# Three edits in a one-core transformer kernel: the last expert's scatter, the squares of an attention, the gate rows of a scan

## The reference, cut to what matters

```python
# first block: for each head and direction, chunk by chunk (here 128 tokens)
logw = where(tril, cum[..., :, None] - cum[..., None, :] + ic[..., None, :], -inf)
m = maximum(inter, logw.max(-1))
s = einsum('bhjd,bhsd->bhjs', qc, kc) * exp(logw - m[..., None])
...
# experts: 16 experts, each takes its 128 best tokens
y = einsum('becf,efd->becd', hid, w_down) * vals[..., None]
return zeros_like(h).at[bidx, idx].add(y)
...
# first attention ("A"): 4 heads, two softmaxes each, then a norm over the 128 values of a head
w = p[:, :, 0] - lam * p[:, :, 1]
o = rms_norm(einsum("bhqk,bkhe->bqhe", w, v), subln_g) * (1.0 - lam_init)
```

## Time and profile before

| | us |
|---|---|
| median of 3 runs | 3016.61 (3014.56 to 3016.85) |
| the profiled execution, its time | 3016.07 |
| its span in the trace | 3014.2 |
| PE busy in it | 2781.5 |
| DVE busy | 1690.4 |
| ACT busy | 1408.7 |

### The profile page before, as it was taken

How to read it: one execution, slowest core, us unless ns; L and a number is a source line. 1 busy time by engine, 2 the same in 40 slices (tenths; PEclk the granted TensorE clock), 3 DMA queues, 4 the chain that set the end, 5 groups by cost and what they waited for, 6 DMA issues and landing times.

```text
span 3014.2 us, 38322 instructions
## 1 busy us (share of the span) xinstructions
PE 2781.5 (92%) x13952; PEld 2070.1 (69%) x13966; DVE 1690.4 (56%) x3155; ACT 1408.7 (47%) x2556; POOL 211.7 (7%) x250
## 2 busy tenths in 40 slices
PE   7999999999993899999978988999999989989998
PEld 3567794788772677777747755675677775866676
DVE  2368363334467788888846468544533556536533
ACT  2343362223242666666636356634632548437421
POOL 0000000000010000000015000000020000000500
PEclk9999999999996999999989999999999999999999
DMA  9510200322434899999965000301041201000321
GB/s 374 190 56 29 102 11 1 135 89 84 156 143 166 306 378 378 377 377 378 377 181 161 17 22 8 85 1 43 23 133 68 86 15 58 29 18 19 113 84 56
DMA packets 178537, 401.33 MB, mean 133 GB/s; under 512 B 7964, under 2 KB 9020, under 8 KB 177872
## 3 DMA queue, kind: packets, MB, share of 16 engines
q1 hardware_dynamic: 158224, 329.27, 30.8%
q0 software_dynamic: 20016, 70.00, 7.2%
q10 hardware_dynamic: 144, 0.01, 0.0%
HBM read 363.44 MB, written 35.81 MB: 132 GB/s over the span
## 4 chain that ended last, share of the span: by engine, by line
PE 80%; DVE 8%; ACT 5%; issue 4%; DMA 3%; POOL 0%; DVEq 0%; POOLq 0%; SPq 0%; ACTq 0%
PE psum L787 7%; PE psum L302 7%; PE psum L789 7%; PE psum L788 7%; PE psum L1490 4%; PE psum L1492 4%; PE psum L1491 4%; PE psum L1625 4%; PE psum L1435 3%; PE psum L1434 3%; PE psum L1433 3%; PE psum L1667 3%; PE psum L1643 3%; PE psum L1728 2%; PE psum L1730 2%
## 5 line engine op out<-in xcount | busy, mean ns | idle before, releaser
L788 PE MATMUL psum<-ring_r,kctx_r 128*128 128x512 f32 (+1 forms) x544 | 214.0, 393 | 0.0
L788 PE MATMUL psum<-ring_r,cols_r 128*128 128x512 f32 (+1 forms) x544 | 213.6, 393 | 0.0
L2136 ACT ACTIVATE ring<-ring,att 128x256 f32<-128x256 f32 (+7 forms) x256 | 173.3, 677 | 72.8 <-DVE att L2774 72.8
L2628 DVE TENSOR_TENSOR ring_r<-ring,pair_r 128x1024 fp32r<-128x1024 f32 x128 | 148.0, 1219 | 51.4 <-ACT pair_r L2014 51.4
L1625 PE MATMUL psum<-wide 64*128 64x512 f32 (+2 forms) x704 | 152.8, 515 | 18.5 <-DVE att L2774 15.5
L1491 PE MATMUL psum<-ring_r,wide_r 128*128 128x512 f32 x384 | 151.3, 394 | 0.0
L626 DVE TENSOR_TENSOR ring_r<-ring,ring_r 128x1024 fp32r<-128x1024 f32 x48 | 58.7, 1225 | 129.7 <-ACT ring_r L623 129.3
L1433 PE MATMUL psum<-small_r,ring_r 128*128 128x512 f32 x320 | 125.8, 393 | 0.8 <-DVE pair L2498 0.8
L1435 PE MATMUL psum<-small_r,ring_r 128*128 128x512 f32 x320 | 126.3, 395 | 0.0
L2014 ACT ACTIVATE pair_r<-ring 128x1024 fp32r<-128x1024 f32 x128 | 124.6, 1049 | 0.0
L788 PEld LDWEIGHTS psum<-ring_r,kctx_r 128*128 128x128 f32 x544 | 104.9, 193 | 22.5
(11 more groups left out here) (557 smaller groups left out, 7185.0 us busy)
## 6 DMA issues: line engine op xcount, KB each, us to landing
ring<-in_w_gate SPq DMA_DIRECT2D x64, 1024.0 KB, 9.5
ring<-in_w_up SPq DMA_DIRECT2D x32, 1024.0 KB, 9.7
hidden<-in_w_up SPq DMA_DIRECT2D x32, 1024.0 KB, 9.6
hidden<-in_w_down SPq DMA_DIRECT2D x32, 1024.0 KB, 8.8
pair<-in_w_down SPq DMA_DIRECT2D x32, 1024.0 KB, 9.0
ring<-in_w_ada SPq DMA_DIRECT2D x24, 1024.0 KB, 14.4
ring<-in_w_in SPq DMA_DIRECT2D x24, 1024.0 KB, 7.3
ring<-in_even_w_in SPq DMA_DIRECT2D x16, 1024.0 KB, 13.6
```

What stands on the lines that cost most here:

```text
L788: self.eng.matmul(outp, XHIGH[b][:, k, :], low[:, k, 0:wd], start=False, stop=False)
```

## The change

It has three parts. (1) The last expert's result goes out in one transfer of full rows, with the same code as the other experts (`one(NEXP, False)`). (2) In attention A ACT squares one block in each step, right after the exponentials (`square(g)`), instead of eight at the end of a head; the square root stays behind the eighth. The sums lie in two halves of `qst`, for even and odd heads. (3) The gate rows are split into a float32r part `r_high` (rows 0 to 35 of `extra`) and the rest `r_low` (rows 64 to 99), and one float32r product with the doubled selector (100 x 128) takes the place of the float32 product with 36 rows. For it the constant `sel` becomes 100 rows high, ACT copies it once to float32r, DVE clears `extra` ahead of the wait for `gates`, and DVE makes `r_low`.

```diff
--- before.py
+++ after.py
@@ -173,14 +173,16 @@
                    ("wide", 9256),
                    ("small", 6500),
                    ("kctx", NH * CTX), ("cols", NCH * 4 * NG),
-                   ("sel_wT", 8 * P), ("lam_f", 448), ("dftc", 2 * P + 1))
+                   ("sel_wT", 8 * P), ("lam_f", 448), ("dftc", 2 * P + 1), ("extra", SEQ))
         with ExitStack() as views:
             split = {n: views.enter_context(nc.sbuf_tensor(n + "_r", [P, c], F32R)) for n, c in REGIONS}
-        ring, hidden, ctx_hidden, pair, wide, small, kctx, cols, sel_wT, lam_f, dftc = (sb(n, c) for n, c in REGIONS)
+        ring, hidden, ctx_hidden, pair, wide, small, kctx, cols, sel_wT, lam_f, dftc, extra = (sb(n, c) for n, c in REGIONS)
         ident = sb("ident", P)
         identb = sb("identb", P, BF16)
         maskb = sb("maskb", 2 * NH * P, BF16)
-        sel = sel_wT[0:NG, :]
+        NB = 64 + NG
+        sel_both = split["sel_wT"][0:NB, :]
+        sel = split["sel_wT"][0:NG, :].bitcast(F32)
         cT = sb("cT", KT * 2)
         adaT = sb("adaT", 2 * 48)
         badaT = sb("badaT", 48)
...
@@ -446,7 +447,7 @@
         se = small[:, 3336:3336 + 1024].rearrange("p (b h n) -> p b h n", b=2, h=NH)
         ee = small[:, 4360:4360 + 1024].rearrange("p (b h n) -> p b h n", b=2, h=NH)
         obs = [small[:, o:o + NH * VW].rearrange("p (h n) -> p h n", h=NH) for o in (5384, 5984)]
-        rRs = extra[0:NG, :]
+        r_high, r_low, r_both = (split["extra"][q, :] for q in (slice(0, NG), slice(64, NB), slice(0, NB)))
         dnb = lam_f[:, 256:256 + 8 * NCH].rearrange("p (c n) -> p c n", c=8)
         rec = small[:, 5980:5984]
         oT = pair[:, 0:4 * D].rearrange("p (h n) -> p h n", h=NH)
...
@@ -935,7 +936,7 @@
         @block.gpsimd
         def _(pool):
             for o, i in ((badaT[:], a["b_adaT"]), (gT[:], a["gT"]), (ident[:], a["ident"]),
-                         (mask_in, a["masks"]), (sel, a["sel"]),
+                         (mask_in, a["masks"]), (sel_wT[0:NB, :], a["sel"]),
                          (dftc[:], a["dftc"]), (wconv[:], a["w_convT"]), (wgate, a["w_mgate"]),
                          (bgate[0:NG, :], a["b_gate"]), (wrt[:], a["w_routerT"])):
                 pool.dma_start(o, i).then_inc(S("const"), 16)
...
@@ -1005,14 +1006,7 @@
             with pool.Fori(1, NEXP - 1) as e:
                 one(e, True)
             one(NEXP - 1, False)
-            for m in range(2):
-                ms = slice(m * HALF, (m + 1) * HALF)
-                pool.wait_ge(S("moe_y"), 2 * NEXP - 1 + m)
-                pool.tensor_scalar(idx1[:, 2 + m:3 + m], idxc[:, NEXP - 1:NEXP], 2, m, ALU.mult, ALU.add)
-                pool.drain()
-                pool.indirect_dma_start(scratch["acc"].rearrange("t (m n) -> (t m) n", m=2), bass.IndirectOffsetOnAxis(idx1[:, 2 + m:3 + m].bitcast(U32), 0), yb[:, ms], None,
-                                        compute_op=ALU.add).then_inc(S("moe_sct"), 16)
-            pool.wait_ge(S("moe_sct"), 16 * NEXP + 16)
+            one(NEXP, False)
             pool.wait_ge(S("gf"), 16)
             for t in range(TT + 1):
                 if t < TT:
...
@@ -1349,6 +1344,7 @@
             pe.wait_ge(S("v_ev"), NCH)
             pe.wait_ge(S("qk_silu"), 2 * NH)
             pe.wait_ge(S("c_zero"), 2)
+            pe.wait_ge(S("r_low"), 1)
 
             def scan_first(i):
 
...
@@ -1365,7 +1361,7 @@
                     pe.wait_ge(S("scan_e"), 4 * no)
                 pe.matmul(bank(1), identb[:], maskb[:, d * NH * P:(d + 1) * NH * P], start=True, stop=False, skip_group_check=True)
                 for h in range(NH):
-                    mm = pe.matmul(bank(1)[:, span(h)], sel[:, (4 * d + h) * P:(4 * d + h + 1) * P], rRs[:, span(c - CT)],
+                    mm = pe.matmul(bank(1)[:, span(h)], sel_both[:, (4 * d + h) * P:(4 * d + h + 1) * P], r_both[:, span(c - CT)],
                                    start=False, stop=(h == NH - 1), skip_group_check=True)
                 mm.then_inc(S("scan_r"), 1)
                 if no >= 1:
...
@@ -1799,6 +1795,7 @@
                     u_act(i - 2)
                 if i % 2 == 0:
                     ada_act(i + 2)
+            act.activation(sel_both, sel_wT[0:NB, :], ACT.Copy).then_inc(S("sel_mm"), 1)
             NC.squares(act, 0)
             NC.squares(act, 1)
             NC.evac_act(act, 0)
...
@@ -1836,7 +1833,7 @@
                     act.wait_ge(S("fu_ev"), 2 * (c - 1))
                 act.activation(sinp[c % 2], bank(2 * (c % 2) + 1), ACT.Copy).then_inc(S("sinp"), 1)
             act.wait_ge(S("gate_rows"), 1)
-            act.activation(rRs, rR[:, CTX:TTOT], ACT.Copy)
+            act.activation(r_high, rR[:, CTX:TTOT], ACT.Copy).then_inc(S("r_high"), 1)
             for c in range(NCH):
                 act.activation(rF[:, span(c)], rI[:, span(c)], ACT.Exp, bias=stat[0:NG, 20 + c:21 + c])
                 act.activation(rC[:, span(c)], rR[:, span(c)], ACT.Exp, bias=stat[0:NG, 40 + c:41 + c])
...
@@ -2148,15 +2145,19 @@
                     act.activation(wT[wT_of(at, t, h)][:, 0:n, :], turned(i)[:, 0:n * P].rearrange("p (k n) -> p k n", k=n),
                                    ACT.Copy).then_inc(S(name + "_wevA"), 1)
 
-                def squares(c):
-                    act.wait_ge(S("A_o"), before("A_o") + at.last[c] + 1)
-                    for b in range(TT):
-                        if c or b:
-                            act.wait_ge(S("A_osq"), TT * c + b)
-                        act.activation(xsq, obuf[c % 2][:, b, :], ACT.Square,
-                                       accum_out=qst[:, b:b + 1]).then_inc(S("A_osq"), 1)
-                    act.wait_ge(S("A_osq"), TT * (c + 1))
-                    act.activation(qst[:, 8:16], qst[:, 0:8], ACT.Sqrt, bias=epsc[:, 0:1], scale=1.0 / (2 * HD)).then_inc(S("A_ort"), 1)
+                def square(g):
+                    c, b = at.pairs[g][0:2]
+                    q = 24 * (c % 2) + b
+                    act.wait_ge(S("A_o"), before("A_o") + g + 1)
+                    if g:
+                        act.wait_ge(S("A_osq"), g)
+                    if c >= 2:
+                        act.wait_ge(S("A_on"), before("A_on") + c - 1)
+                    act.activation(xsq, obuf[c % 2][:, b, :], ACT.Square, accum_out=qst[:, q:q + 1]).then_inc(S("A_osq"), 1)
+                    if g == at.last[c]:
+                        q = 24 * (c % 2)
+                        act.wait_ge(S("A_osq"), TT * (c + 1))
+                        act.activation(qst[:, q + 8:q + 16], qst[:, q:q + 8], ACT.Sqrt, bias=epsc[:, 0:1], scale=1.0 / (2 * HD)).then_inc(S("A_ort"), 1)
 
                 def mix(c):
                     i = at.turns["fin", c]
...
@@ -2173,8 +2174,8 @@
                         exponentials(e, (1,))
                     if t is not None and at.heads == 2:
                         empty(t, 1)
-                    if name == "A" and at.ended(i, 0) is not None:
-                        squares(at.ended(i, 0))
+                    if name == "A" and u is not None:
+                        square(u)
                     for c in fins:
                         mix(c)
                 act.wait_ge(S(name + "_trD"), before(name + "_trD") + at.wide0[-1])
...
@@ -2355,6 +2356,7 @@
             for t in range(TT):
                 ss.tokens(t)
             link(dve.memset(ones_row, 1.0))
+            link(dve.memset(split["extra"][:].bitcast(F32), 0.0))
             dve.wait_ge(S("gates"), 1)
             link(dve.tensor_scalar(rM, rM, 0.0, None, ALU.min))
             link(dve.tensor_tensor(rF, rM, rC, ALU.subtract))
...
@@ -2405,6 +2407,8 @@
                 dve.tensor_tensor(fuT[:, c, HALF + 1:D][:, ::-1], cosp[:, 1:HALF], half[:, 1:HALF], ALU.subtract).then_inc(S("fu_ev"), 1)
             dve.wait_ge(S("fu_mm"), 5)
             dve.tensor_copy(fuT[:, :, HALF], bank(7)[:, 0:4]).then_inc(S("fu_ev"), 1)
+            dve.wait_ge(S("r_high"), 1)
+            dve.tensor_tensor(r_low, rR[:, CTX:TTOT], r_high.bitcast(F32), ALU.subtract).then_inc(S("r_low"), 1)
             cols_dve(range(NCH))
             dve.wait_ge(S("dn_mm"), before("dn_mm") + 1)
             dve.tensor_copy(dnb, bank(6)[:, 0:8 * NCH].rearrange("p (c n) -> p c n", c=8)).then_inc(S("dn"), 1)
...
@@ -2824,10 +2828,12 @@
 
                 def complete(c):
 
+                    q = 24 * (c % 2)
+                    r = qst[:, q + 16:q + 24]
                     dve.wait_ge(S("A_ort"), c + 1)
-                    link(dve.reciprocal(qst[:, 16:24], qst[:, 8:16]))
+                    link(dve.reciprocal(r, qst[:, q + 8:q + 16]))
                     for b in range(TT):
-                        ins = dve.tensor_scalar(obuf[c % 2][:, b, :], obuf[c % 2][:, b, :], qst[:, 16 + b:17 + b], None, ALU.mult)
+                        ins = dve.tensor_scalar(obuf[c % 2][:, b, :], obuf[c % 2][:, b, :], r[:, b:b + 1], None, ALU.mult)
                     ins.then_inc(S("A_on"), 1)
 
                 def mix(c):
...
@@ -2997,6 +3003,7 @@
```

(23 more changed lines are left out.)

## The result

| | before | after |
|---|---|---|
| median | 3015.59 us (4 runs, 3013.44 to 3016.85) | 2994.18 us (4 runs, 2993.02 to 2996.55) |
| span of the profiled execution | 3014.2 us | 2993.2 us |

The ratio is 0.9927, interval 0.9912 to 0.9942: 22.0 us less by the ratio, between 17.5 and 26.5 (the two medians are 21.4 apart). Forecast were 16.5 less and a time from 2996 to 3012. The kernel is faster, as forecast, and faster than the range allowed.

The account below looks back on a forecast made before the run. PE was taken to bound the scan, with DVE's gate chain on the path ahead of it. Terms -10.3 - 5.0 - 2.5 + 0.6 + 0.7 = -16.5 against 3016.07 made 2999.6, say 3000 us; range 2996 to 3012.

Parts of the forecast that it names:

- the rivals: Short float32r product no faster, 3010.4 (0.33); only the scan gives, 3007.6 (0.10); squares hold up wide steps, 3023 (0.05).
- A: Scan: a short float32r product is no faster than a float32 one, the scan gives 0, 3010.4; chance 0.33.
- Squares, -5.0: Attention A, heads' ends: seven of eight squares go earlier, 1.7 us at each of three ends; bounds 3.2 and 8.2.
- Gate rows on PE, -10.3: Scan: four products per output step fall from 1.08 to 0.44 us, 0.64 saved in each of 16 steps.
- That the saving passes on: Scan: L2460 ends 1.6 us ahead, ACT idles 1.73 a step, so PE stays the bound, period 4.87.
- Its cost ahead, +1.3: Setup ahead of the scan: 0.6 us for DVE's clear and up to 0.7 for the larger selector transfer.
- The clear's 0.6: DVE's clear of `extra` before the wait for `gates` makes PE's wait at L1291 0.6 us longer; bounds 0 and 1.2.
- The selector's 0.7: At the start: the selector's transfer grows from 36 to 100 rows, 262 KB more at 394 GB/s, up to 0.7 us.
- The moved squares cost nothing, narrowly: Attention A, steps with 1024 keys: slack 1.6 us before L2797, use 1.4, 0.2 left; no added table loads.
- Scatter, -2.5: Last expert: one full transfer issued at 1564.9 instead of a second half at 1569.89, 2.5 us gained; bounds 0.4 and 5.0.
- The range: Whole kernel: 2996 to 3012 us, top reaching the float32r rival's 3010.4, bottom the scan's floor with a little of the scatter's.
- the scan's floor as -3: Scan: at 0.06 us per product 16 steps save 13.4 instead of 10.3 us, taken as -3 for the range's bottom.

Follow-up runs that it names:

- scan only: Only the scan's part (float32r products, selector of 100 rows, clear, split) put on the kernel before; 3007.28 us, ratio 0.9966.
- squares only: Only the squares moved block by block into the steps of attention A, on the kernel before; 3009.44 us, ratio 0.9969.

## Why the forecast was right or wrong

The sign and the bound (PE in the scan, the setup ahead of it) were right, and the scatter is the least gain, as forecast; scan and squares are not apart in time. The size was not: 16.5 forecast, 22.0 measured. None of the rivals occurred, A (0.33, a short float32r product as dear as a float32 one) least of all. By the runs of single parts the 5.5 between them lie with the squares (9.4 for 5.0) and with the gate rows and their setup (10.3 for 9.0). Step by step:

- **Squares, -5.0.** The step that failed is "a shorter one also leaves less of the stretch at the 0.50 clock, but DVE has work of its own there. I take 1.7 per end". It put the clock at next to nothing and took the waits too dear. Alone in time the part gave 9.4, over its bound of 8.2. At like clock an end gave 1.08, DVE's wait and no more, 3.3 for three, at the lower bound; PE's own wait behind L2148 is gone there, but from ahead of the first end (1780 us in the trace of before) to behind it (1815 us) PE's starts gain only 1.1 us from scan only to squares only, at a clock of 1.00 in both. The other 4 to 6 us came with a higher granted clock, in attention A and behind it (mean over the execution 0.969 for 0.967). That moving the squares brings it is shown by the run with the squares alone; that it does so through PE's shorter waits is argued, not isolated. The two errors had opposite signs.
- **Gate rows on PE, -10.3.** The second step that failed is "a step saves 1.08 - 0.44 = 0.64". The price of the new product was nearly right (0.40; the quarter of the old price, 0.27, was not reached). Missing was the neighbour: the score products behind became 0.15 shorter, because the product in front no longer has 36 rows. A step saves 0.84. PE's starts moved by 11.9 us over the scan, not by 16 x 0.84 = 13.4: in front of the second step with an output PE waits 0.80 us for ACT, which loads a table at that point. That the saving passes on was right; ACT still idles 1.17 in a step.
- **Its cost ahead, +1.3.** The clear's 0.6 was right: PE's wait went from 3.66 to 4.26. The selector's 0.7 can't be confirmed: PE's starts near 118 us are 0.9 late in the trace after, but against the same trace of before 0.2 late in its second one, 1.1 in the two other traces with the small selector, and between 0.0 and 1.4 in those with the large one, but for one with 3.4. The 3.3 us beyond it were never the change's: the trace of before had drawn a stretch at 2.4 GHz that none of the others had.
- **The moved squares cost nothing, narrowly.** Right; 0.3 us were left in a wide step.
- **Scatter, -2.5.** The issue time was right. The landing, 6.1 us where 7.5 was taken, made it 4.1 by the trace. The term's mechanism held, its size did not, and inside its bound of 5.0. The time of this part alone, 2.4 with an interval of 3.3 to each side, does not show even the sign.
- **The range.** Its low end took the scan's floor as -3 and next to nothing from the squares and the scatter, though the text had bounds of 3.2 and 2.5 us further for these. Three terms whose bounds all reach lower make a longer lower side than one.

What stays open: why the granted clock is higher with moved squares, also behind attention A; why a product of 36 rows costs its full-height neighbours time, and where between 36 and 100 rows the price changes. Other heights were not tried. Nor is it known what decides whether an execution has the stretch at 1.2 GHz ahead of 195 us: of fourteen traces one had none, the others means between 0.74 and 0.91 in that window.

## What to carry to other kernels

When a cheap product sits between full-height ones, price it with its neighbours: read the chain over the whole step, since a product with few rows can cost as much in the next group as in its own. Before a stretch of the trace is compared across two kernels, look whether both ran it at the same granted clock, and take a second trace of the unchanged kernel; here one lucky stretch looked like a cost of 3.3 us in the change. End a window at an instruction on the path of the engine that bounds; here 3.0 of 5.0 us stood at a reciprocal that PE did not wait for. Add the bounds of all terms for a range, also on the side where you hope.

## What was not expected of the hardware

- Float32 products over 100 rows ran in 0.89 us for four, over 36 rows in 1.08; the float32 products of 128 rows behind them in 0.89 and 1.09.
- With the squares of attention A moved, the mean clock of an execution was 0.969 for 0.967, and a stretch at 1.2 GHz some 65 us behind them was gone in eight of ten traces.
- The same instructions behind the same wait of 3.66 us ran once at 2.4 GHz and once at 1.2 GHz in two executions of the same kernel, and all that follows came 4.3 to 4.8 us later.
- An indirect transfer of 128 rows of 4 KB with nothing beside it landed in 6.1 us, half rows (2 KB) in 6.9 with the first half still on its way; among the experts the full one took 8.5 to 9.9, most often 8.6.
